# The MLP's up projection with the high and low part of x side by side

## Chip, cores and metric

One core of a Trainium2 chip runs the whole program. The metric is the device time of one execution in microseconds (us), as the median of several runs.

## The reference, cut to what matters

Two decoder layers work on x, 256 tokens of 1024 channels, in float32. The end of each layer is a squared-ReLU MLP with 4096 hidden channels:

```
hm = rmsnorm(x, norm_mlp[l])
x = x + jnp.square(jax.nn.relu(hm @ w_up[l])) @ w_down[l]
```

Before it stand the token mixers (a state-space branch, two attentions, gates, an output projection) and a cross attention. The state-space branch of the second layer needs tables that depend on parameters alone; the kernel computes them during the first layer's MLP.

## The kernel before

**Split products.** Each float32 matrix and each activation is split into a high part (rounded to `fp32r`) and a low part (the rest). A product is the sum of three: high x high, high x low, low x high (helper `three`, L1819 to L1821).

**Units and chunks.** All weights go through one pipeline. A unit is two chunks of 128 x 1024 values. SyncE loads a chunk into `raw`, ScalarE (ACT) rounds it into `w_hi` (L898), VectorE (DVE) subtracts to get `w_lo` (L1295), TensorE (PE) multiplies. `prep(u)` makes both chunks of a unit. `w_hi` has four slots, so ACT can round a chunk only once the chunk four places back (two units) has been multiplied.

**The MLP.** `up(g)` is two units, `("up", g, 0)` and `("up", g, 1)`; each makes 256 hidden channels for 256 tokens: 8 row tiles of x times 2 column tiles of the weights (`ft`) is 16 places, three matmuls of 256 columns each, 48 in all. `down(g)` is two units of 24 matmuls of 512 columns. The order is up(0), up(1), down(0), up(2), down(1), ..., up(7), down(6), down(7): 16 up and 16 down units a layer. In this text unit n is counted from up(0) = units 0 and 1; so up(1) is 2 and 3, up(2) 6 and 7, up(3) 10 and 11, up(4) 14 and 15, up(5) 18 and 19, up(6) 22 and 23, up(7) 26 and 27, and the rest are down units.

**Emptying an up unit.** The two column tiles of an up unit lie side by side in one PSUM bank, T0 for the first unit of a pair and T1 for the second. ACT copies the bank with Relu into `r_b` (which frees the bank), DVE squares it into `q_b`, ACT rounds that into `bT_hi`, DVE subtracts into `bT_lo`. ACT waits for the square inside the step, with everything else of ACT queued behind it.

**Order on the engines.** Each engine runs a list fixed by the program. For unit u of the MLP, ACT and DVE first prepare unit u + 2 and then empty unit u; after that come the side stages attached to u (`side_stages`). In the first layer's MLP these make the second layer's tables: `p_ct` after unit 10, `p_cv` (DVE) after 12 and 13, `p_b0` (DVE) after 15, `p_bv` (DVE) after 16 and 18, `p_k` after 20 and 21 (96 small PE matmuls into bank X0 after unit 20, 16 small ACT copies to `kt`, half after unit 20 and half after 21, the last of which frees X0), and `p_bt` after 22, 23, 24 and 25 (two each time: four PE transposes into X0 or X1, then an ACT copy that frees it). GpSimd (POOL) works on the same tables. The second layer's MLP has no side stages.

**Banks.** `USES` lists the users of a bank in program order, and `before` makes each user wait until the one ahead has freed the bank (on PE, ahead of its first matmul).

Of the kernel before, what the change touches and what calls it, by code (L numbers as in the profile page):

```python
# [30 lines left out]
P = 128  # L31
# [95 lines left out]
def side_stages(l):  # L127

    side = {u: [] for u in range(-1, NU)}

    def after(u, *stage):
        side[u].append(stage)

    up0 = AT_UNIT["up", 0, 0]
    if l:
        after(-1, "turn_x", "mix", 0)
        after(-1, "turn_x", "mix", 1)
    after(-1, "norm", "mix")
    if l == 0:
        after(-1, "p_dt", 0)  # L140
    after(-1, "stats", "mix", 0)
    after(-1, "stats", "mix", 1)
    if l == 0:
        after(-1, "p_angle", 0)
        after(-1, "p_cos", 0)
        after(2, "lam", 0)
        after(3, "lam", 1)
        after(4, "p_params", 0)
    after(1, "row")

    def pre(tgt, u):

        after(u["ct"], "p_ct", tgt)
        for r in range(2):
            after(u["cv"][r], "p_cv", tgt, r)
        after(u["b0"], "p_b0", tgt)
        for r in range(2):
            after(u["bv"][r], "p_bv", tgt, r)
        for n in range(2):
            after(u["k"][n], "p_k", tgt, n)  # L160
        for n in range(8):
            after(u["bt"][n // 2], "p_bt", tgt, n)

    if l == 0:
        pre(0, dict(ct=0, cv=(1, 2), b0=3, bv=(4, 5), k=(5, 6), bt=(6, 7, 7, 8)))
        first = FIRST[0]
        after(up0 + 6, "p_params", 1)
        after(up0 + 7, "p_dt", 1)
        after(up0 + 7, "p_angle", 1)
        after(up0 + 8, "p_cos", 1)  # L170
        pre(1, dict(ct=up0 + 10, cv=(up0 + 12, up0 + 13), b0=up0 + 15, bv=(up0 + 16, up0 + 18),
                    k=(up0 + 20, up0 + 21), bt=(up0 + 22, up0 + 23, up0 + 24, up0 + 25)))
    else:
        first = FIRST[1]
    for kb in range(4):
        after(first + kb, "ssm_in", kb)
        after(first + 2 + kb, "ssm_out", kb)
    after(first + 6, "gelu")
    after(first + 9, "gelu_split")

    for p in range(SB_PAIRS):
        after(6 + 2 * p, "sb_s", p)
        after(7 + 2 * p, "sb_u", p)
        after(8 + 2 * p, "sb_p", p)
    after(10, "rope", 0)
    after(15, "turn", 0)
    after(12, "rope", 1)
    after(15, "turn", 1)

    for j in range(2 * DA_HEADS):  # L190
        after(16 + j, "da_s", j)
        after(17 + j, "da_t", j)
        after(18 + j, "da_p", j)
    after(21, "da_c", 0)
    after(22, "da_n", 0)
    after(25, "da_o", 0)
    after(25, "da_c", 1)
    after(25, "da_n", 1)
    after(27, "da_o", 1)
    if l == 0:  # L200
        after(32, "stats", "mem", 0)
        after(32, "stats", "mem", 1)
    after(33, "mem_diag")
    after(34, "mem_row")
    for j in range(4):
        after(34 + j // 2, "mem_split", j)
    after(AT_UNIT["wout", 1], "stats", "cross", 0)
    after(AT_UNIT["wout", 3], "stats", "cross", 1)
    after(AT_UNIT["wout", 3], "turn_x", "cross", 0)
    after(AT_UNIT["xk", 0], "turn_x", "cross", 1)  # L210
    after(AT_UNIT["xk", 0], "norm", "cross")

    xq = AT_UNIT["xq", 0]
    for h in range(XA_HEADS):
        after(xq + h // 2, "xa_s", h)
        after(xq + 1 + h // 2, "xa_t", h)
    for h in range(XA_HEADS):
        after(xq + h // 2, "xa_w", h)
    for h in range(XA_HEADS):
        after(xq + 3, "xa_p", h)  # L220
    after(AT_UNIT["xo", 0], "stats", "mlp", 0)
    after(AT_UNIT["xo", 1], "turn_x", "mlp", 0)
    after(AT_UNIT["xo", 1], "turn_x", "mlp", 1)
    after(AT_UNIT["xo", 1], "norm", "mlp")
    after(AT_UNIT["xo", 1], "stats", "mlp", 1)
    for u in range(7, 27):
        side[u].sort(key=lambda s: RANK.get(s[0], 7))
    return side
# [12 lines left out]
def unit_banks(key):  # L241

    if key[0] == "u":
        return [["A0", "A2"][key[1]]]
    if key[0] in ("sq", "sk", "xk", "xq") or isinstance(key[0], tuple):
        return ["T0", "T1"][key[1] % 2:][:1]
    if key[0] in ("sv", "dq", "dk", "dv", "xv"):
        return ["T0", "T1"]
    if key[0] == "glu":
        return ["T0", "T1"] if key[1] else ["A0", "A1"]  # L250
    if key[0] == "branch":
        return {1: ["T0", "T1"], 2: ["A0", "A1"], 0: ["A2", "A3"]}[key[2]]
    if key[0] == "wout":
        return ["A0", "A1"] if key[1] < 2 else ["A2", "A3"]
    if key[0] == "xo":
        return ["A2", "A3"] if key[1] == 0 else ["A0", "A1"]
    if key[0] == "up":
        return ["T0", "T1"][key[2]:][:1]
    return ["A0", "A1"] if key[2] == 0 else ["A2", "A3"]


# [104 lines left out]
def hybrid_trunk(nc, a, out):  # L366
    with ExitStack() as ctx:
# [20 lines left out]
        raw = [nc.alloc_sbuf_tensor_at(f"s_raw{i}", [P, CW], F32, offset=ring + 4 * CW * i) for i in range(LO)]  # L388
        w_hi = [sb(f"w_hi{i}", [P, CW], F32R) for i in range(HI)]
        x = sb("x", [P, NT, D])  # L390
        hT_hi, hT_lo = sb("hT_hi", [P, KD, T], F32R), sb("hT_lo", [P, KD, T], F32R)

        bT_hi, bT_lo = sb("bT_hi", [P, 12, T], F32R), sb("bT_lo", [P, 12, T], F32R)
        gates = sb("gates", [P, 16, T])
# [117 lines left out]
        xmax_ready, xw_ready = signal("xmax_ready", XA_HEADS), signal("xw_ready", XA_HEADS)  # L512
        xo_hi = signal("xo_hi", XA_HEADS)
        NUP = 2 * (HIDDEN // 512)
        sq_made, hid_hi, hid_ready = signal("sq_made", NUP), signal("hid_hi", NUP), signal("hid_ready", NUP)

        act_order, dve_order, pool_order = sem("act_order"), sem("dve_order"), sem("pool_order")
# [24 lines left out]
        def f32(ap):  # L542
            return ap.bitcast(F32)
# [36 lines left out]
        def by_place(ap):  # L580

            return ap.rearrange("p (k b j) -> p k j b", b=NB, j=BL)

        def by_block(ap):
            return ap.rearrange("p (k j b) -> p k j b", b=NB, j=BL)
# [310 lines left out]
        def _(act):  # L896
# [6 lines left out]
            for l in range(DEPTH):  # L903
# [121 lines left out]
                def evac(u):  # L1025
# [29 lines left out]
                    elif key == ("glu", 0):  # L1055
                        gated(1)
                        fn(flat(gates[:, 0:8, :]), flat(gates[:, 0:8, :]), ACT.Sigmoid).then_inc(*st.sig(gate_ready))
                        for j, bk in enumerate(b):
                            act.wait_ge(*st.at(*freed(l, bk, key)))
                            fn(flat(hT_hi[:, 2 * j:2 * j + 2, :]), st_y[:, 0, 512 * j:512 * j + 512]).then_inc(*st.sig(glu_hi))  # L1060
                    elif kind == "branch":
                        cb, n = key[1:]
                        if cb == 0 and n == 1:
# [7 lines left out]
                        if n == 0:  # L1071
                            for j in range(2):
                                act.wait_ge(*st.at(mg_made, 2 * cb + j + 1))
                                fn(flat(merged(cb)[0][:, 2 * j:2 * j + 2, :]), macc(cb, j)).then_inc(*st.sig(mg_hi))
                    elif kind == "xq":
                        take(flat(qk[:, 2 * key[1]:2 * key[1] + 2, :]), b[0], key)
                    elif kind == "up":
                        g, i = key[1:]
                        if g:
                            act.wait_ge(*st.at(sq_made, 2 * g + i - 1))  # L1080
                        take(r_b[i], b[0], key, ACT.Relu)
                        act.wait_ge(*st.at(sq_made, 2 * g + i + 1))
                        if g >= 2:

                            act.wait_ge(*st.at(chunk_done, 2 * AT_UNIT["down", g - 2, 1] + 2))
                        k0 = 4 * (g % 2) + 2 * i
                        fn(flat(bT_hi[:, k0:k0 + 2, :]), q_b[i]).then_inc(*st.sig(hid_hi))
# [162 lines left out]
        def _(dve):  # L1250
# [39 lines left out]
            for l in range(DEPTH):  # L1290
# [230 lines left out]
                def evac(u):  # L1521
# [36 lines left out]
                    elif key == ("glu", 0):  # L1558
# [5 lines left out]
                                .then_inc(*st.sig(*freed(l, bk, key)))  # L1564
                        for j in range(2):
                            dve.wait_ge(*st.at(glu_hi, j + 1))
                            tt(flat(hT_lo[:, 2 * j:2 * j + 2, :]), st_y[:, 0, 512 * j:512 * j + 512],
                                      f32(flat(hT_hi[:, 2 * j:2 * j + 2, :])), ALU.subtract)\
                                          .then_inc(*st.sig(glu_ready))
                    elif kind == "branch":  # L1570
                        cb, n = key[1:]
# [15 lines left out]
                        if n == 0:  # L1587
                            for j in range(2):
                                dve.wait_ge(*st.at(mg_hi, 2 * cb + j + 1))
                                hi, lo = merged(cb)  # L1590
                                tt(flat(lo[:, 2 * j:2 * j + 2, :]), macc(cb, j),
                                          f32(flat(hi[:, 2 * j:2 * j + 2, :])), ALU.subtract)\
                                              .then_inc(*st.sig(mg_ready))
                    elif kind in ("wout", "xo", "down"):
                        residual(key, b)
                    elif kind == "up":
                        g, i = key[1:]
                        dve.wait_ge(*st.at(*freed(l, b[0], key)))
                        tt(q_b[i], r_b[i], r_b[i]).then_inc(*st.sig(sq_made))
                        dve.wait_ge(*st.at(hid_hi, 2 * g + i + 1))  # L1600
                        k0 = 4 * (g % 2) + 2 * i
                        tt(flat(bT_lo[:, k0:k0 + 2, :]), q_b[i], f32(flat(bT_hi[:, k0:k0 + 2, :])),
# [197 lines left out]
        def _(pe):  # L1800
# [14 lines left out]
            for l in range(DEPTH):  # L1815
# [48 lines left out]
                def unit(u, late):  # L1864
# [10 lines left out]
                    for half in range(2):  # L1875
# [4 lines left out]
                        if kind == "T":  # L1880
# [3 lines left out]
                            for k, ft in order:  # L1884
# [3 lines left out]
                                elif after_norm and ft == 0 and ks % 2 == 0:  # L1888
                                    pe.wait_ge(*st.at(*freed(l, TURN_BANKS[ks // 2], ("turn_x", after_norm, ks // 4))))
                                c = slice(ft * P, ft * P + P)  # L1890
                                o = bank[banks[ft // 2]][:, (ft % 2) * T:(ft % 2) * T + T]
                                ins = three(o, wh[:, k, c], wl[:, k, c], hi[:, ks, :], lo[:, ks, :],
                                            half == 0 and k == 0 and ft % 2 == 0, half == 1 and k == kt // 2 - 1,
# [272 lines left out]
```

## Time and profile before

| what | value |
|---|---|
| median of 3 runs | 1093.74 us (1093.61 to 1093.97) |
| the profiled execution's own time | 1096.48 us |
| its span in the trace | 1094.8 us |
| PE busy | 1029.5 us (94%) |
| DVE busy | 736.7 us (67%) |
| ACT busy | 573.4 us (52%) |
| first layer's MLP on PE | 376.4 to 568.5 us |
| second layer's MLP on PE | 905.5 us to near the end |

The span runs from the first to the last instruction of the trace; the own time is 1.7 us longer. A matmul's row is longer than its share of PE, since matmuls overlap: what one costs is the distance from its start to the next one's.

### The profile page before, as it was taken

How to read it: one execution, taken by the hardware profiler on the slowest of the kernel's cores; microseconds unless marked ns; L12 is line 12 of the kernel's file. 1: busy time of each engine (PE TensorE's matmuls, PEld its weight loads, DVE VectorE, ACT ScalarE, POOL GpSimd, SP SyncE). 2: the span in 40 equal slices, each digit the busy share in tenths (PEclk: the TensorE clock that was granted, in tenths of full speed). 3: DMA queues.
4: the chain of work that ended last, by engine and by line, in shares of the span. 5: the costliest groups of instructions: out<-in, count | busy, mean ns of one | idle time of the engine just before them, and what ended most of it. 6: DMA issues, size and time to landing. Idle time of an engine off the chain costs nothing. (4 is left out here: it accounts for less than half of the span.)

```text
span 1094.8 us, 18335 instructions
## 1 busy us (share of the span) xinstructions
PE 1029.5 (94%) x7096; PEld 937.9 (86%) x7096; DVE 736.7 (67%) x1061; ACT 573.4 (52%) x868; POOL 176.7 (16%) x304
## 2 busy tenths in 40 slices
PE   5778999999999899999989999999999989999996
PEld 4766889989998799988979878998998979899995
DVE  4884975878875565887465579478787647555554
ACT  6446445546765555546554454554637546444442
POOL 5993300000000003997000011000000000000000
PEclk9889999999999999999999999999999999999998
DMA  7253336645554366654556543465565445666661
GB/s 281 97 173 95 98 120 194 201 141 174 176 175 149 96 232 182 189 172 136 172 173 189 163 130 97 135 213 154 155 181 175 146 135 160 190 189 192 182 188 74
DMA packets 58022, 177.21 MB, mean 162 GB/s; under 512 B 14160, under 2 KB 16208, under 8 KB 57680
## 3 DMA queue, kind: packets, MB, share of 16 engines
q1 hardware_dynamic: 57792, 176.04, 52.2%
q8 instruction: 57, 0.93, 0.3%
q14 instruction: 29, 0.24, 0.1%
q10 hardware_dynamic: 144, 0.00, 0.0%
HBM read 172.87 MB, written 3.15 MB: 161 GB/s over the span
## 5 line engine op out<-in xcount | busy, mean ns | idle before, releaser
L1295 DVE TENSOR_TENSOR s_w_lo<-s_raw,s_w_hi 128x1024 fp32r<-128x1024 f32 x312 | 377.3, 1238 | 146.7 <-ACT s_w_hi L898 143.0
L898 ACT ACTIVATE s_w_hi<-s_raw 128x1024 fp32r<-128x1024 f32 x312 | 321.0, 1054 | 215.2 <-PE p_T L1821 130.5
L1819 PE MATMUL p_T<-s_hT_hi,s_w_hi 128*128 128x256 f32 x1088 | 313.4, 288 | 12.0 <-DVE s_w_lo L1295 11.9
L1820 PE MATMUL p_T<-s_hT_lo,s_w_hi 128*128 128x256 f32 x1088 | 310.0, 285 | 0.0
L1821 PE MATMUL p_T<-s_hT_hi,s_w_lo 128*128 128x256 f32 x1088 | 309.7, 285 | 0.0
L1819 PEld LDWEIGHTS p_T<-s_hT_hi,s_w_hi 128*128 128x128 f32 x1088 | 210.7, 194 | 17.6 <-issue 16.2
L1820 PEld LDWEIGHTS p_T<-s_hT_lo,s_w_hi 128*128 128x128 f32 x1088 | 210.8, 194 | 0.4
L1821 PEld LDWEIGHTS p_T<-s_hT_hi,s_w_lo 128*128 128x128 f32 x1088 | 210.9, 194 | 0.0
L1819 PE MATMUL p_A<-s_w_hi,s_bT_hi 128*128 128x512 f32 x320 | 125.2, 391 | 2.4 <-DVE s_bT_lo L1295 2.4
L1820 PE MATMUL p_A<-s_w_lo,s_bT_hi 128*128 128x512 f32 x320 | 124.7, 390 | 0.0
L1821 PE MATMUL p_A<-s_w_hi,s_bT_lo 128*128 128x512 f32 x320 | 124.6, 389 | 0.0
L1819 PEld LDWEIGHTS p_A<-s_w_hi,s_bT_hi 128*128 128x128 f32 x320 | 60.1, 188 | 15.2 <-issue 3.2
L1821 PEld LDWEIGHTS p_A<-s_w_hi,s_bT_lo 128*128 128x128 f32 x320 | 60.1, 188 | 12.7
L1820 PEld LDWEIGHTS p_A<-s_w_lo,s_bT_hi 128*128 128x128 f32 x320 | 60.1, 188 | 11.7
L727 POOL TENSOR_TENSOR s_small<-s_small 128x16 f32<-128x16 f32 (+1 forms) x130 | 59.8, 483 | 10.2 <-ACT s_small L898 7.8
L1819 PE MATMUL p_T<-s_w_hi,s_hT_hi 128*128 128x512 f32 x128 | 52.2, 408 | 8.0 <-issue 8.0
L898 ACT ACTIVATE s_bT_hi<-s_att 128x512 fp32r<-128x512 f32 x32 | 20.2, 632 | 58.5 <-DVE s_att L1295 58.5
L1821 PE MATMUL p_T<-s_w_hi,s_hT_lo 128*128 128x512 f32 x128 | 50.8, 397 | 0.0
L1820 PE MATMUL p_T<-s_w_lo,s_hT_hi 128*128 128x512 f32 x128 | 50.7, 396 | 0.0
L727 POOL TENSOR_TENSOR s_small<-s_col,s_small 128x16 f32<-128x16 f32 x4 | 1.2, 313 | 296.7 <-ACT s_small L898 296.7
L1819 PE MATMUL p_A<-s_hT_hi,s_w_hi 128*128 128x256 f32 x128 | 37.8, 295 | 9.5 <-DVE s_hT_lo L1394 9.5
L1819 PE MATMUL p_T<-s_bT_hi,s_w_hi 128*128 128x256 f32 x160 | 45.9, 287 | 0.3 <-issue 0.3
(263 smaller groups left out, 1685.5 us busy)
## 6 DMA issues: line engine op xcount, KB each, us to landing
s_raw<-in_weights SPq DMA_DIRECT2D x312, 512.0 KB, 3.6
s_bt<-in_mem_t SPq DMA_DIRECT2D x2, 1024.0 KB, 6.1
s_st_y<-in_x_t SPq DMA_DIRECT2D x2, 512.0 KB, 6.9
s_x<-in_x SPq DMA_DIRECT2D x1, 1024.0 KB, 10.6
s_vN<-in_ssm_bc SPq DMA_DIRECT2D x2, 512.0 KB, 8.9
u_turn<-s_st_y SPq DMA_DIRECT2D x4, 256.0 KB, 3.8
s_uB<-u_turn SPq DMA_DIRECT2D x8, 128.0 KB, 3.4
s_bt<-in_mem SPq DMA_DIRECT2D x1, 1024.0 KB, 5.9
```

Source lines behind the costliest of these rows:

```text
L727: return nc.gpsimd.tensor_tensor(o, i0, i1, op)
L898: return nc.scalar.activation(o, i, f, **kw)
L1295: return V.tensor_tensor(o, i0, i1, op)
L1819: mm(o, lhi, rhi, start=first, stop=False, **kw)
L1820: mm(o, lhi, rlo, start=False, stop=False, **kw)
L1821: return mm(o, llo, rhi, start=False, stop=last, **kw)
```

## The change

`hT_hi` and `hT_lo` become two halves of one tile, so that for each of the 8 row tiles of x the high and the low part of its 256 tokens are 512 neighbouring columns. In an up unit each place has two products in place of three: `w_hi` times both parts (512 columns, a whole bank), and `w_lo` times the high part (256 columns, added to the bank's first half). The result is the sum of the two halves of the bank. So each column tile needs a bank of its own: the first unit of a pair takes T0 and T1, the second X0 and X1. Emptying: ACT copies the second half of each bank (256 columns each, no Relu) into `r_b`, DVE adds the first half of each bank to it (which frees the bank) and then takes max(r, 0) times r in one `scalar_tensor_tensor`. As X0 and X1 have other users, the stage `p_bt` moves from after units 22, 23, 24, 25 to after 24, 25, 28, 29. All else keeps its order; some access patterns are written in three dimensions for the new tile.

```
 pre(1, ...
-        bt=(up0 + 22, up0 + 23, up0 + 24, up0 + 25)))
+        bt=(up0 + 24, up0 + 25, up0 + 28, up0 + 29)))
 unit_banks:
-        return ["T0", "T1"][key[2]:][:1]
+        return ["T0", "T1"] if key[2] == 0 else ["X0", "X1"]
 tiles:
-        hT_hi, hT_lo = sb("hT_hi", [P, KD, T], F32R), sb("hT_lo", [P, KD, T], F32R)
+        hT = sb("hT", [P, KD, 2, T], F32R)
+        hT_hi, hT_lo = hT[:, :, 0, :], hT[:, :, 1, :]
 ACT, evac of "up":
-        take(r_b[i], b[0], key, ACT.Relu)
+        act.wait_ge(*st.at(chunk_done, 2 * u + 2))
+        for j, bk in enumerate(b):
+            ins = fn(r_b[i][:, j * T:j * T + T], bank[bk][:, T:2 * T])
+            ins.then_inc(*st.sig(up_copied)) if j else ins.then_inc(*st.mid())
         act.wait_ge(*st.at(sq_made, 2 * g + i + 1))
 DVE, evac of "up":
-        dve.wait_ge(*st.at(*freed(l, b[0], key)))
-        tt(q_b[i], r_b[i], r_b[i]).then_inc(*st.sig(sq_made))
+        dve.wait_ge(*st.at(up_copied, 2 * g + i + 1))
+        for j, bk in enumerate(b):
+            tt(r_b[i][:, j * T:j * T + T], r_b[i][:, j * T:j * T + T], bank[bk][:, 0:T], ALU.add)\
+                .then_inc(*st.sig(*freed(l, bk, key)))
+        dve.wait_ge(*st.mine())
+        V.scalar_tensor_tensor(out=q_b[i], in0=r_b[i], scalar=0.0, in1=r_b[i], op0=ALU.max, op1=ALU.mult)\
+         .then_inc(*st.sig(sq_made))
 PE, unit:
+        if key[0] == "up":
+            o = bank[banks[ft]]
+            mm(o[:, :], wh[:, k, c], hT[:, ks, :, :].rearrange("p r n -> p (r n)"),
+               start=(half == 0 and k == 0), stop=False, skip_group_check=True)
+            ins = mm(o[:, 0:T], wl[:, k, c], hi[:, ks, :], start=False,
+                     stop=(half == 1 and k == kt // 2 - 1), skip_group_check=True)
+            continue
```

## Rows read from the trace of the kernel before

**Rows 1.** Page, engines: busy us (share of the span) xinstructions.
```profile
PE 1029.5 (94%) x7096; PEld 937.9 (86%) x7096; DVE 736.7 (67%) x1061; ACT 573.4 (52%) x868; POOL 176.7 (16%) x304
```

**Rows 2.** Windows of the MLPs: length, then busy us (xcount) of each engine, clock, DMA.
```profile
core 0: us, PE busy (x) PEld busy (x) DVE busy (x) ACT busy (x) POOL busy (x), PEclk, DMA share, GB/s
444.00:504.00 60.00, 58.21 (x430) 51.09 (x429) 52.97 (x54) 26.43 (x32) 57.80 (x80) 1.00 0.58 170
905.00:1063.00 158.00, 157.94 (x1060) 146.37 (x1059) 92.31 (x100) 78.78 (x98) 0.00 (x0) 1.00 0.61 183
```

**Rows 3.** Timeline, PE, second layer: first matmul of up, down and up again.
```profile
939.48 0.28 PE L1819 MATMUL p_T<-s_hT_hi,s_w_hi 128*128 128x256 f32 x1
...
950.99 0.40 PE L1819 MATMUL p_A<-s_w_hi,s_bT_hi 128*128 128x512 f32 x1
...
961.89 0.28 PE L1819 MATMUL p_T<-s_hT_hi,s_w_hi 128*128 128x256 f32 x1
```

**Rows 4.** Groups by line and shape: xcount, busy us, mean ns, idle before.
```profile
L1295 DVE TENSOR_TENSOR s_w_lo<-s_raw,s_w_hi 128x1024 fp32r<-128x1024 f32 x312 | 377.3, 1238 | 146.7 <-ACT s_w_hi L898 143.0 <-DVE s_att L1295 0.6 <-DVE s_w_lo L1295 0.6
L1295 DVE TENSOR_TENSOR s_att<-s_att 128x512 f32<-128x512 f32 x36 | 24.8, 688 | 0.5 <-DVE s_w_lo L1295 0.4
...
L1295 DVE TENSOR_TENSOR s_att<-p_X,s_masks 128x256 f32<-128x256 f32 x32 | 12.8, 420 | 8.6 <-PE p_X L1998 5.3 <-PE p_X L2032 2.7 <-DVE s_vN L1535 0.4
...
L1713 DVE SCALAR_TENSOR_TENSOR s_att<-s_att 128x768 f32<-128x768 f32 x8 | 8.0, 1005 | 6.9 <-ACT s_att L898 6.9
...
L1295 DVE TENSOR_TENSOR s_att<-s_vN,s_small 128x768 f32<-128x768 f32 x4 | 3.7, 963 | 3.4 <-POOL s_small L727 3.2
...
L898 ACT ACTIVATE s_att<-p_T 128x512 f32<-128x512 f32 x32 | 18.5, 579 | 0.0
...
L898 ACT ACTIVATE s_bT_hi<-p_A 128x256 fp32r<-128x256 f32 x16 | 6.1, 383 | 6.1 <-PE p_A L2089 5.8
```

**Rows 5.** Timeline, DVE, first layer's MLP; s_att rows are the squares of up units.
```profile
386.02 0.69 DVE L1295 TENSOR_TENSOR s_att<-s_att 128x512 f32<-128x512 f32 x1
...
445.92 2.38 DVE L1295 TENSOR_TENSOR s_w_lo<-s_raw,s_w_hi 128x1024 fp32r<-128x1024 f32 x2 [2.65 <-ACT s_w_hi L898]
448.23 0.70 DVE L1295 TENSOR_TENSOR s_att<-s_att 128x512 f32<-128x512 f32 x1
...
465.55 0.71 DVE L1295 TENSOR_TENSOR s_att<-s_att 128x512 f32<-128x512 f32 x1
...
470.29 0.70 DVE L1295 TENSOR_TENSOR s_att<-s_att 128x512 f32<-128x512 f32 x1
...
489.50 0.69 DVE L1295 TENSOR_TENSOR s_att<-s_att 128x512 f32<-128x512 f32 x1
...
500.76 0.70 DVE L1295 TENSOR_TENSOR s_att<-s_att 128x512 f32<-128x512 f32 x1
```

**Rows 6.** Timeline, ACT: rounding after p_ct; the second half of p_k's copies.
```profile
444.73 2.01 ACT L898 ACTIVATE s_w_hi<-s_raw 128x1024 fp32r<-128x1024 f32 x2
...
509.71 3.61 ACT L898 ACTIVATE s_kt<-p_X 32x512 f32<-32x512 f32 x8
```

**Rows 7.** Timeline, PE: units 18, p_k, 21, 22, p_bt, p_bt, 24.
```profile
478.05 0.36 PE L1819 MATMUL p_T<-s_hT_hi,s_w_hi 128*128 128x256 f32 x1 [0.20 <-DVE s_w_lo L1295]
...
497.01 0.64 PE L1931 MATMUL p_X<-s_ct,s_tmp 128*32 128x128 f32 x16
...
500.08 0.50 PE L1819 MATMUL p_A<-s_w_hi,s_bT_hi 128*128 128x512 f32 x1
...
505.66 0.28 PE L1819 MATMUL p_T<-s_hT_hi,s_w_hi 128*128 128x256 f32 x1
...
513.47 1.06 PE L1804 MATMUL p_X<-s_ident,s_gates 128*128 128x128 f32 x8 [1.90 <-ACT s_kt L898]
...
521.61 1.03 PE L1804 MATMUL p_X<-s_ident,s_gates 128*128 128x128 f32 x8
522.40 0.48 PE L1819 MATMUL p_A<-s_w_hi,s_bT_hi 128*128 128x512 f32 x1
```

**Rows 8.** Window of unit 23, columns as in rows 2.
```profile
514.00:522.00 8.00, 8.00 (x57) 8.00 (x56) 4.95 (x5) 4.98 (x8) 1.09 (x2) 0.79 0.27 89
```

More of the change, by code:

```diff
@@ L171, in side_stages @@
         pre(1, dict(ct=up0 + 10, cv=(up0 + 12, up0 + 13), b0=up0 + 15, bv=(up0 + 16, up0 + 18),
-                    k=(up0 + 20, up0 + 21), bt=(up0 + 22, up0 + 23, up0 + 24, up0 + 25)))
+                    k=(up0 + 20, up0 + 21), bt=(up0 + 24, up0 + 25, up0 + 28, up0 + 29)))
     else:
@@ L514, in hybrid_trunk @@
         NUP = 2 * (HIDDEN // 512)
+        up_copied = signal("up_copied", NUP)
         sq_made, hid_hi, hid_ready = signal("sq_made", NUP), signal("hid_hi", NUP), signal("hid_ready", NUP)
@@ L582, in by_place, with by_tile @@
             return ap.rearrange("p (k b j) -> p k j b", b=NB, j=BL)
+        def by_tile(ap):
+            return ap.rearrange("p (k n) -> p k n", n=T)
         def by_block(ap):
@@ L1059, in evac @@
                             act.wait_ge(*st.at(*freed(l, bk, key)))
-                            fn(flat(hT_hi[:, 2 * j:2 * j + 2, :]), st_y[:, 0, 512 * j:512 * j + 512]).then_inc(*st.sig(glu_hi))
+                            fn(hT_hi[:, 2 * j:2 * j + 2, :], by_tile(st_y[:, 0, 512 * j:512 * j + 512])).then_inc(*st.sig(glu_hi))
                     elif kind == "branch":
@@ L1073, in evac @@
                                 act.wait_ge(*st.at(mg_made, 2 * cb + j + 1))
-                                fn(flat(merged(cb)[0][:, 2 * j:2 * j + 2, :]), macc(cb, j)).then_inc(*st.sig(mg_hi))
+                                fn(merged(cb)[0][:, 2 * j:2 * j + 2, :], by_tile(macc(cb, j))).then_inc(*st.sig(mg_hi))
                     elif kind == "xq":
@@ L1566, in evac @@
                             dve.wait_ge(*st.at(glu_hi, j + 1))
-                            tt(flat(hT_lo[:, 2 * j:2 * j + 2, :]), st_y[:, 0, 512 * j:512 * j + 512],
-                                      f32(flat(hT_hi[:, 2 * j:2 * j + 2, :])), ALU.subtract)\
+                            tt(hT_lo[:, 2 * j:2 * j + 2, :], by_tile(st_y[:, 0, 512 * j:512 * j + 512]),
+                                      f32(hT_hi[:, 2 * j:2 * j + 2, :]), ALU.subtract)\
                                           .then_inc(*st.sig(glu_ready))
@@ L1590, in evac @@
                                 hi, lo = merged(cb)
-                                tt(flat(lo[:, 2 * j:2 * j + 2, :]), macc(cb, j),
-                                          f32(flat(hi[:, 2 * j:2 * j + 2, :])), ALU.subtract)\
+                                tt(lo[:, 2 * j:2 * j + 2, :], by_tile(macc(cb, j)),
+                                          f32(hi[:, 2 * j:2 * j + 2, :]), ALU.subtract)\
                                               .then_inc(*st.sig(mg_ready))
```

## The prediction

> **What bounds the kernel now.** I read the page's first part, then the windows of the two MLPs, then PE's timeline there, and last the timelines of DVE and ACT where PE has gaps. PE is busy for 94% of the span, DVE for 67% [rows 1]. That average hides two kinds of stretch. In the second layer's MLP, PE is busy for 157.94 of 158 us while DVE works 92.31 [rows 2]: the distance between matmuls alone sets the pace. In the first layer's MLP from 444 to 504 us, DVE is busy for 52.97 of 60 us [rows 2]; what is left are pauses of about 0.7 us in which it waits for ACT's rounding of an up unit. There DVE, with the table work, is the bound, and PE shows it: unit 18 is held for `w_lo` [rows 7]. So each edit must be asked twice, once where PE paces and once where DVE does.
>
> **Part 1, PE's matmuls.** Two up units are 96 matmuls of 256 columns and take 950.99 - 939.48 = 11.51 us, 119.9 ns each; two down units are 48 of 512 columns and take 961.89 - 950.99 = 10.90 us, 227.1 ns each [rows 3]. Two narrow ones cost 239.8, so a matmul has a fixed part of 239.8 - 227.1 = 12.7 ns, and that is all the change takes away: a place costs 227.1 + 119.9 = 347.0 ns after 359.7. An up unit has 16 places: 0.20 us. The columns stay what they were. All 32 up units would give 6.5 us. Bounds: 512-wide matmuls right after a narrow stretch start a little dearer (PE needs 505.66 - 500.08 = 5.58 us for the 24 of unit 21 [rows 7], 232.5 ns each), which would leave 7.3 ns a place; if the fixed part went altogether, a place would gain 38 ns. I take 12.7, since both widths show it over dozens of matmuls with a weight load each.
>
> A page speaks against this term. The Trainium skill, "TensorE: Matmul & The Clock Gate", section "Back-to-back issue gap", gives N / 2.4 + 2.5 ns for an isolated matmul with N columns at full clock. By it a place would gain 2.5 ns and the 32 units 1.3 us. The trace does not agree: 119.9 ns for 256 columns, where the page's form gives 109.2. It stands as a rival below.
>
> **Part 2, DVE's work per up unit.** Before: one square of 512 elements, 688 ns. After: two additions of 256 elements with one operand in PSUM, and one `scalar_tensor_tensor` of 512. The nearest row for an addition is 420 ns (256 elements from PSUM). Instructions in a row overlap by about 0.1 us (two `w_lo` take 2.38 [rows 5], one 1.238 [rows 4]), so the pair takes 0.74. The third must wait for the second's result; 0.03 for that. A `scalar_tensor_tensor` of 768 elements takes 1005 ns where a plain one takes 963 [rows 4]: 0.04 more. So 0.8 us more DVE time per up unit. Below, 0.5: the additions at half a square each, overlapping fully with what surrounds them. Above, 1.1: the additions stretched as `w_lo` is in places while POOL works. ACT has two copies of 383 ns, overlapping, for one of 579 [rows 4]: 0.1 us more, hidden behind DVE's `w_lo`, which ends later.
>
> **Part 3, second layer.** An up unit takes PE 5.56 us, and DVE needs 2 x 1.19 (`w_lo`), 0.7 + 0.8, the 0.7 pause and 0.7 (`bT_lo`), 5.3 in all; after two up units two down units follow with 2.4 us each, so DVE falls behind by little and catches up, two units ahead of need. No wait appears. A new wait on banks is possible only at the start, where up(1) needs T0 and T1 one unit after up(0) filled them. In the first layer the square of unit 0 starts at 386.02 [rows 5]; additions there would be done by 386.8, and unit 2 starts at 387.6. It passes. Second layer: 16 x 0.20 = -3.2 us.
>
> **Part 4, first layer up to p_k.** PE gains 0.20 in each of units 0, 1, 2, 3, 6, 7, 10: it is 1.4 us early at the end of unit 10. From there on the order of ACT and DVE counts. Emptying unit 10 costs 0.8 more, so ACT reaches `p_ct` and then the rounding of 444.73 [rows 6] 0.6 early, and DVE starts the `w_lo` of 445.92 [rows 5] 0.6 early. From there to 500.76 DVE has no slack that a later PE or ACT could give back. Each emptying puts 0.8 on it: unit 11 (448.23) makes it 0.2 late, unit 14 (465.55) 1.0, unit 15 (470.29) 1.8, unit 18 (489.50) 2.6 [rows 5]. The emptying of unit 19 then starts at 500.76 + 2.6 = 503.4. PE's own gains in units 11 to 19 are worth nothing here: unit 18 starts 1.8 late, at about 479.9 after 478.05 [rows 7], with PE idle for some 4 us.
>
> **Part 5, the new wait.** `p_k` writes X0 on PE after unit 20, and X0 now has a user just ahead: unit 19, up(5)'s second. Before, PE began `p_k` at 497.01 [rows 7], 3.7 us before the square of unit 19 even began. Now it must wait for unit 19's first addition, which ends at 503.4 + 0.4 = 503.8. PE reaches that point near 498.7 (unit 19 can start at 487.5, when its `w_lo` is made, then 5.6 and 5.5 us) and stands for about 5 us. Queued behind it are unit 21 and all that follows. `p_k` takes 500.08 - 497.01 = 3.1 us [rows 7]. After such a pause the clock is low for a while: in the window of unit 23, which follows a pause of 1.90 us [rows 7], it was 0.79 of full over 8 us, so 8 x 0.21 = 1.7 us were lost [rows 8]. What a low clock costs `p_k`'s small matmuls no row shows: between 0.2 and 1.8 us in all; I take 1.0. Unit 21 starts at 503.8 + 3.1 + 1.0 = 507.9, where it started at 500.08.
>
> **Part 6, from unit 21 on.** Before, PE waited again: from the end of unit 22 to 513.47 for ACT's copies of `p_k` [rows 6, 7], and then ran unit 23 slow. This wait goes: the copies of the second half end about when unit 22 does. So units 21, 22, 23 follow closely, 5.6 us each: unit 23 ends at 507.9 + 16.7 = 524.6 after 521.61 [rows 7], 3.0 late. The step of `p_bt` takes 522.40 - 521.61 = 0.8 us each time [rows 7]; before, three of four came after this point, now all four: +0.8. Units 26 and 27 give back 0.4. X0 and X1 are free in time for unit 27 (the copies of 0.6 us run beside unit 26) and for the stages after 28 and 29. Late at the layer's end: 3.0 + 0.8 - 0.4 = 3.4 us.
>
> **Sum.** +3.4 - 3.2 = +0.2 us. The profiled execution of 1096.48 us (span 1094.8) would become 1096.7. It lies 2.7 us above the median of the runs shown; on the median the same difference gives 1094.0 us.
>
> **Rivals.**
>
> *A, the gain comes through.* The additions hide in the pauses and `p_k`'s wait is short. For it: DVE's share is 67%, and pauses of 0.7 us stand beside each emptying. Against: those pauses wait for ACT's rounding, which waits for the very step that grows. In full: -6.5 us, 1087.2. Chance 0.12.
>
> *B, the wait at p_k costs more than the fixed part brings.* Its place is X0 between units 19 and 21. An emptying at 1.1 us puts 5 x 0.3 = 1.5 us on the chain, and a low clock through `p_k` and the start of unit 21 another 0.8: +2.5 us, 1096.2. It decides once unit 21 starts later than about 509.9. For it: POOL is busy for 57.80 of these 60 us [rows 2] beside DVE. Chance 0.29.
>
> *C, a matmul's fixed part is not saved.* By the page's 2.5 ns, or because a wide matmul in this mix is dearer, as in unit 21, the second layer gives 0.6 in place of 3.2, and the chain begins 0.3 early in place of 1.4, with 0.3 more for units 26 and 27: +4.2 us, 1097.9. Chance 0.05.
>
> The forecast has the remaining 0.54.
>
> **How the numbers follow.** A measurement of this kernel tells 0.2% (2.2 us) from no change. Below 1091.6 lie A with 0.12 and the low end of my own sum (emptying 0.5 us, which takes 1.5 off, and a place gaining more than 12.7 ns) with 0.09: faster 0.21. Above 1095.9 lie most of B (0.25), C (0.05) and 0.02 of the forecast: slower 0.32. Same: 0.47. The likeliest case alone runs from 1091.9 (0.5 us, low clock 0.2) to 1095.6. The range leaves out most of A, the upper end of C: 1091.0 to 1097.6.
>
> **What would show it.** In the second layer's MLP, two up units at 11.1 us after 11.51, with no wait on PE: part 1 and 3. If they are near 11.4, C is right. In the first layer, PE waiting several us ahead of L1931's counterpart for DVE's write of `s_att`: part 5; no such wait, and A is right. The start of unit 23 with no wait for `s_kt`: part 6. Four additions near 0.42 us for each pair of units: part 2. The prediction is wrong if the first layer's MLP ends within 1 us of its old place or more than 6 us late.

## The result and the profile after

The changed kernel takes 1100.91 us (median of 4 runs, 1100.23 to 1102.26) against 1093.86 for before: ratio 1.0064, 95% interval 1.0046 to 1.0081. It is slower by 0.6%. The forecast was no change at 1094.0 us; the time lies outside its range, which ended at 1097.6.

The profiled execution took 1102.26 us, with a span of 1100.2 us against 1094.8 before: 5.4 us more. The page's first part stands beside [rows 1]:

```profile
PE 1029.2 (94%) x6584; PEld 911.6 (83%) x6584; DVE 760.3 (69%) x1125; ACT 574.4 (52%) x900; POOL 176.5 (16%) x304
```

512 matmuls fewer, PE's busy time as before, DVE busy for 24 us more. Where the span grew is read from PE's timeline. In each execution I take two lengths: the first layer's MLP from its first up matmul to the first transpose of x behind it, and the second layer's from its first up matmul to the first matmul of down(6), which follows the last up unit.

| stretch | before | changed | difference |
|---|---|---|---|
| first layer's MLP | 192.06 us | 198.17 us | +6.1 us |
| second layer's MLP (up to down(6)) | 157.62 us | 155.68 us | -1.9 us |

The MLP starts 1.0 us later in this execution; that belongs to no stage of the change (over all the kernels below, whose programs are alike up to there but for the tile of x's parts, this start lies anywhere from 375.3 to 378.3 us). The stages sum to +4.2 us of the 5.4, and with the later start to 5.2; the stretch between the two MLPs (337.0 and 337.2 us) and the one behind them (31.7 in both) are as before.

**Second layer.** Timeline of PE, changed kernel: first matmul of two up units, then of the down unit behind them. It answers to [rows 3].

```profile
946.04 0.39 PE L1906 MATMUL p_T<-s_hT,s_w_hi 128*128 128x512 f32 x1
...
957.33 0.40 PE L1832 MATMUL p_A<-s_w_hi,s_bT_hi 128*128 128x512 f32 x1
```

11.29 us for two up units, after 11.51: 0.11 us a unit gained, where 0.20 was forecast.

**DVE's longer emptying.** Groups by line and shape of the changed kernel, DVE and ACT (xcount, busy us, mean ns, idle before), to set beside [rows 4]:

```profile
L1611 DVE SCALAR_TENSOR_TENSOR s_att<-s_att 128x512 f32<-128x512 f32 x32 | 22.7, 710 | 1.1
...
L1303 DVE TENSOR_TENSOR s_att<-s_att,p_X 128x256 f32<-128x256 f32 x32 | 11.9, 414 | 0.0
...
L903 ACT ACTIVATE s_att<-p_T 128x256 f32<-128x256 f32 x32 | 10.2, 373 | 0.0
```

An addition takes 414 ns where 420 was estimated, and the last operation 710 ns, 22 over the square of before (688) where 40 was estimated.

**First layer.** Timeline of PE in the changed kernel: start of unit 18, of `p_k`, of units 21, 22, 23 and 24 [compare rows 7]; the bracket is the idle time before and what ended it.

```profile
481.48 0.47 PE L1906 MATMUL p_T<-s_hT,s_w_hi 128*128 128x512 f32 x1 [3.65 <-DVE s_w_lo L1303]
...
504.94 0.87 PE L1951 MATMUL p_X<-s_ct,s_tmp 128*32 128x128 f32 x12 [4.45 <-DVE s_att L1303]
...
510.04 0.80 PE L1832 MATMUL p_A<-s_w_hi,s_bT_hi 128*128 128x512 f32 x1
...
516.83 0.39 PE L1906 MATMUL p_T<-s_hT,s_w_hi 128*128 128x512 f32 x1
...
522.47 0.40 PE L1906 MATMUL p_X<-s_hT,s_w_hi 128*128 128x512 f32 x1
...
528.12 0.40 PE L1832 MATMUL p_A<-s_w_hi,s_bT_hi 128*128 128x512 f32 x1
```

The wait that was forecast ahead of `p_k` is there, 4.45 us long and ended by DVE's write of `s_att`. DVE's timeline has what ended it, the first of unit 19's two additions [compare the last of rows 5]:

```profile
504.39 0.74 DVE L1303 TENSOR_TENSOR s_att<-s_att,p_X 128x256 f32<-128x256 f32 x2
```

But `p_k` then takes 510.04 - 504.94 = 5.1 us, and unit 21 516.83 - 510.04 = 6.8 us; before they took 3.1 and 5.6. The windows of these stretches, columns as in [rows 2], show why:

```profile
505.00:510.00 5.00, 5.00 (x96) 3.15 (x96) 4.07 (x5) 2.52 (x3) 4.92 (x4) 0.50 0.01 3
510.00:513.00 3.00, 3.00 (x16) 2.36 (x9) 2.04 (x1) 2.64 (x6) 2.88 (x2) 0.55 0.00 0
```

The granted clock is 0.50 in `p_k`, the lower of TensorE's two levels, and still 0.55 in the first 3 us of unit 21.

### The profile page after: what moved, and what is told of

The parts are those of the page before. It is cut to its first block and busy times, and to the rows that moved or that the text cites. A ratio compares the mean times of both kernels' runs of the same rounds, so it can differ in the third digit from the quotient of the medians.

```text
span 1100.2 us, 17437 instructions
## 1 busy us (share of the span) xinstructions
PE 1029.2 (94%) x6584; PEld 911.6 (83%) x6584; DVE 760.3 (69%) x1125; ACT 574.4 (52%) x900; POOL 176.5 (16%) x304
## 5 line engine op out<-in xcount | busy, mean ns | idle before, releaser
L1832 PE MATMUL p_T<-s_hT,s_w_hi 128*128 128x256 f32 x576 | 167.0, 290 | 9.4 <-DVE s_w_lo L1303 9.4
L1833 PE MATMUL p_T<-s_hT,s_w_hi 128*128 128x256 f32 x576 | 163.8, 284 | 0.0
L1834 PE MATMUL p_T<-s_hT,s_w_lo 128*128 128x256 f32 x576 | 163.8, 284 | 0.0
L1832 PEld LDWEIGHTS p_T<-s_hT,s_w_hi 128*128 128x128 f32 x576 | 111.3, 193 | 13.6 <-issue 12.5
L1833 PEld LDWEIGHTS p_T<-s_hT,s_w_hi 128*128 128x128 f32 x576 | 111.5, 194 | 0.1
L1834 PEld LDWEIGHTS p_T<-s_hT,s_w_lo 128*128 128x128 f32 x576 | 111.3, 193 | 0.0
L1906 PE MATMUL p_T<-s_hT,s_w_hi 128*128 128x512 f32 x256 | 92.5, 403 | 3.8 <-DVE s_w_lo L1303 3.7
L1906 PE MATMUL p_X<-s_hT,s_w_hi 128*128 128x512 f32 x256 | 90.8, 397 | 0.3 <-DVE s_w_lo L1303 0.3
L1908 PE MATMUL p_T<-s_hT,s_w_lo 128*128 128x256 f32 x256 | 72.5, 283 | 0.0
L1908 PE MATMUL p_X<-s_hT,s_w_lo 128*128 128x256 f32 x256 | 71.8, 281 | 0.0
L1906 PEld LDWEIGHTS p_T<-s_hT,s_w_hi 128*128 128x128 f32 x256 | 48.8, 190 | 16.3 <-issue 4.6
L1832 PE MATMUL p_T<-s_w_hi,s_hT 128*128 128x512 f32 x128 | 52.4, 409 | 9.5 <-issue 9.5
```

The source lines that it names most:

```text
L1832: mm(o, lhi, rhi, start=first, stop=False, **kw)
L1833: mm(o, lhi, rlo, start=False, stop=False, **kw)
L1834: return mm(o, llo, rhi, start=False, stop=last, **kw)
L1906: mm(o[:, :], wh[:, k, c], hT[:, ks, :, :].rearrange("p r n -> p (r n)"), start=(half == 0 and k == 0), stop=False, skip_group_check=True)
L1908: ins = mm(o[:, 0:T], wl[:, k, c], hi[:, ks, :], start=False, stop=(half == 1 and k == kt // 2 - 1), skip_group_check=True)
```

## The experiments

My theory after the traces had three parts. DVE's additions make its queue late in the stretch where it is the bound. Bank X0 makes PE stand in that queue ahead of `p_k`. The low clock behind that wait costs 3.2 us. The rivals were that one of these alone explains it, or the new places do. All kernels are compared with before; the columns at the right are from their profiled executions.

| kernel | ratio to before (95%) | first MLP, us | second MLP, us |
|---|---|---|---|
| before | 1 | 192.06 | 157.62 |
| changed | 1.0064 (1.0046 to 1.0081) | 198.17 | 155.68 |
| e1_place | 1.0001 (0.9987 to 1.0016) | 192.16 | 157.61 |
| e2_dvework | 1.0060 (1.0044 to 1.0075) | 196.74 | 157.61 |
| e3_fill | 1.0024 (1.0014 to 1.0034) | 194.79 | 156.09 |
| e4_pklate | 1.0035 (1.0022 to 1.0048) | 196.38 | 155.67 |
| e5_l1only | 0.9985 (0.9975 to 0.9995) | 192.12 | 156.03 |
| e6_most | 0.9990 (0.9976 to 1.0003) | 191.70 | 156.09 |
| e7_l0only | 1.0079 (1.0063 to 1.0094) | 198.32 | 157.62 |
| e8_grouped | 1.0043 (1.0027 to 1.0060) | 196.68 | 155.31 |
| e9_after_bv | 1.0024 (1.0012 to 1.0035) | 192.89 | 156.08 |
| e10_before_bv | 0.9980 (0.9971 to 0.9990) | 188.54 | 157.62 |
| e11_most_grouped | 0.9983 (0.9974 to 0.9993) | 190.00 | 155.20 |
| e12_most_bv | 0.9951 (0.9938 to 0.9963) | 187.94 | 155.30 |

**e1_place: the banks and the moved stage without the rest.**

```
-        return ["T0", "T1"][key[2]:][:1]
+        return ["T0", "X0"][key[2]:][:1]
-        bt=(up0 + 22, up0 + 23, up0 + 24, up0 + 25)
+        bt=(up0 + 24, up0 + 25, up0 + 28, up0 + 29)
```

> The kernel before with the new places alone: the second up unit of a pair fills one bank X0 in place of T1, and p_bt stands after units 24, 25, 28, 29. Matmuls, ACT's Relu and DVE's square are as before. Theory (the loss needs both DVE's longer emptying and the bank X0): ACT's Relu frees X0 near 493.5 us, before PE reaches p_k near 497, so there is no wait ahead of p_k; the time is within 1 us of before. Rival (the places themselves cost, as more users queue on X0): PE waits ahead of p_k or p_bt for X0, and it is 4 us or more slower.

Measured: ratio 1.0001, first MLP 192.16 us. PE starts `p_k` at 496.96 with no wait, so the new places cost nothing by themselves. The wait for ACT's copies of `p_k` that before had ahead of `p_bt` stands now ahead of unit 23, 1.84 us after 1.90.

**e2_dvework: DVE's work without the rest.**

```
-                        tt(q_b[i], r_b[i], r_b[i])
+                        for j in range(2):
+                            half = r_b[i][:, j * T:j * T + T]
+                            tt(half, half, half, ALU.max).then_inc(*st.mid())
+                        dve.wait_ge(*st.mine())
+                        V.scalar_tensor_tensor(out=q_b[i], in0=r_b[i], scalar=0.0, in1=r_b[i], op0=ALU.max, op1=ALU.mult)
```

> The kernel before with DVE's longer emptying alone: two extra in-place operations of 256 elements (a max of r_b with itself, all in SBUF) ahead of the square, and the square as scalar_tensor_tensor. Banks, matmuls and stages as before. Theory (DVE is the bound between 446 and 501 us of the first layer, 0.8 us for each of six emptyings): unit 18 waits about 3 us longer, ACT's copies of p_k end about 5 us later, the first layer's MLP is 4 to 6 us longer, the second layer's unchanged: +5 us. Rival (the additions hide beside PE, and the loss comes from the bank): within 1 us of before.

Measured: ratio 1.0060, first MLP +4.7 us, second unchanged at 157.61. Timeline of PE: unit 18 and the first `p_bt`.

```profile
481.29 0.55 PE L1824 MATMUL p_T<-s_hT_hi,s_w_hi 128*128 128x256 f32 x1 [3.68 <-DVE s_w_lo L1295]
...
518.94 0.74 PE L1809 MATMUL p_X<-s_ident,s_gates 128*128 128x128 f32 x5 [2.45 <-ACT s_kt L898]
```

Unit 18's wait is 3.68 us, in the changed kernel 3.65, before 0.20: that part of the loss is DVE's work alone. The 4.7 us are even a low figure: behind the 2.45 us wait the clock stayed at 1.00 and unit 23 took 5.84 us, where before it fell behind a wait of 1.90 us and the same unit took 7.32 (521.61 - 514.29 [rows 7]). The window of unit 23 in e2_dvework, columns as in [rows 2]:

```profile
519.76:525.60 5.84, 5.84 (x52) 5.84 (x51) 4.42 (x6) 3.41 (x6) 0.00 (x0) 1.00 0.29 80
```

So DVE's work is the larger part of the loss; the new banks put a dearer wait ahead of `p_k`, but they also do away with the one ahead of unit 23. The second layer, with the same additions and no table work, does not feel them.

**e3_fill: PE at work in place of the wait.** Ahead of the wait for X0 in `p_k` of the second table:

```
+                        if t == 1:
+                            pe.wait_ge(*st.at(*freed(l, "T0", ("up", 5, 0))))
+                            for _ in range(20):
+                                mm(bank["T0"][:, :], hT_hi[:, 0, 0:P], hT[:, 0, :, :].rearrange("p r n -> p (r n)"), ...)
                         pe.wait_ge(*st.at(*before(l, b, s)))
```

> The changed kernel with 20 matmuls of 512 columns into the empty bank T0 ahead of p_k's wait for X0, so that PE is at work in place of waiting for 4.45 us; their result is not used. Theory (a low clock after the wait made p_k take 5.1 us after 3.1, and unit 21 6.8 after 5.6): p_k takes 3.1 and unit 21 5.6 us, and the kernel is 3.2 us faster than the changed one, about 3.8 us slower than before. Rival (the small matmuls of p_k are slow for another reason, as being late among POOL's and DVE's work): p_k and unit 21 stay as they are, and so does the time.

Measured: ratio 1.0024 after 1.0064, which is 4.4 us where 3.2 were expected; the first MLP is 3.4 us shorter than in the changed kernel. Timeline of PE: the added matmuls, `p_k`, unit 21, unit 22.

```profile
498.99 0.62 PE L1950 MATMUL p_T<-s_hT 128*128 128x512 f32 x2
...
503.62 0.65 PE L1956 MATMUL p_X<-s_ct,s_tmp 128*32 128x128 f32 x16
...
506.69 0.50 PE L1832 MATMUL p_A<-s_w_hi,s_bT_hi 128*128 128x512 f32 x1
...
512.26 0.39 PE L1906 MATMUL p_T<-s_hT,s_w_hi 128*128 128x512 f32 x1
```

`p_k` takes 3.07 and unit 21 5.57 us, both as before. Nothing else that unit 21 waits for was changed, and `p_k` starts 0.15 us earlier, counted from the MLP's start. So the low clock cost 5.10 - 3.07 and 6.79 - 5.57, 3.2 us in all: shown.

**e4_pklate: p_k away from unit 19.**

```
-        k=(up0 + 20, up0 + 21), bt=(up0 + 24, up0 + 25, up0 + 28, up0 + 29)
+        k=(up0 + 24, up0 + 25), bt=(up0 + 28, up0 + 29, up0 + 30, up0 + 30)
```

> The changed kernel with p_k moved from after units 20 and 21 to after 24 and 25, and p_bt to after 28, 29, 30, 30, so that unit 19's emptying does not stand ahead of p_k. Theory: no wait ahead of p_k; units 19 to 23 follow w_lo alone, unit 23 ends 7 to 8 us earlier; p_k's 3.1 us come later, and two pairs of p_bt in a row cost about 1 us: 3 to 4 us faster than the changed kernel, 3 to 4 us slower than before. Rival (DVE's late work alone sets this stretch, the bank only shows it): the wait moves to w_lo of units 21 and 22, and the time stays within 1 us of the changed kernel's.

Measured: ratio 1.0035, first MLP 1.8 us shorter than in the changed kernel; 3 to 4 were expected. The wait ahead of `p_k` is gone, and another has come ahead of unit 21:

```profile
502.62 0.47 PE L1832 MATMUL p_A<-s_w_hi,s_bT_hi 128*128 128x512 f32 x1 [2.58 <-DVE s_w_lo L1303]
```

The low clock came with it. Window of unit 21, from its first matmul to unit 22's, columns as in [rows 2]:

```profile
502.62:509.77 7.15, 7.14 (x24) 5.72 (x25) 6.22 (x7) 3.48 (x4) 6.99 (x5) 0.76 0.25 76
```

7.15 us, where unit 21 took 5.58 before. And one of the `p_bt` now waits 1.05 us for ACT. So both readings hold in part: the bank made the wait longer, but DVE's queue stands behind it, holds PE at the next `w_lo`, and the clock falls there too.

**e5_l1only, e6_most, e7_l0only: the change in one part of the up units.** A function chooses the form, and both forms stand in the code:

```
+def wide_up(l, g):
+    return l == 1                # e5;  e6: l == 1 or g <= 2;  e7: l == 0
-        return ["T0", "T1"] if key[2] == 0 else ["X0", "X1"]
+        if not wide_up(l, key[1]):
+            return ["T0", "T1"][key[2]:][:1]
+        return ["T0", "T1"] if key[2] == 0 else ["X0", "X1"]
```

(`p_bt` is where it was in e5 and e6, and as in the changed kernel in e7.)

> The change in the second layer alone; the first layer's up units, banks and stages are as before (with the new tile for x's parts). Theory (a place gains 6.8 ns on PE, measured in the changed kernel, and where PE paces DVE's additions are free): 16 units x 0.11 us, 1.8 us faster than before, and the first layer's MLP takes as long as before. Rival (the second layer's gain is eaten by something at its edges, or the new tile costs elsewhere): no faster than before.

> The change in the second layer and in the first layer's up(0) to up(2), that is in all up units before DVE becomes the bound; p_bt where it was. Theory: 22 units x 0.11 us, 2.4 us faster than before, no wait ahead of p_k. Rival (three longer emptyings before the bound stretch delay the tables' start): the first layer gives back its 0.6 us and it equals the kernel with the second layer alone.

> The change in the first layer alone. Theory: the whole loss stands here, so it is the changed kernel without the second layer's gain: 1.8 us slower than that, about 8.8 us slower than before. Rival (part of the loss is in the second layer or in the tile's layout): less than 7 us slower than before.

Measured: the second layer alone is 0.15% faster (0.9985, 0.9975 to 0.9995), its MLP 1.6 us shorter, the first layer's as before. The first layer alone is slower than the whole change (1.0079), with a first MLP of 198.32 us. The loss is all there, as expected. e6 shortens the first MLP by 0.4 us of the 0.7 expected and has no wait ahead of `p_k`; its time, 0.9990 (0.9976 to 1.0003), can't be told from before or from e5.

**e8_grouped: the order of wide and narrow matmuls.**

```
                                     mm(o[:, :], wh[:, k, c], hT[:, ks, ...], ...)
+                                    lows = [(k, ks)]
+                                    if not after_norm:
+                                        lows = [(q, s0 + half * (kt // 2) + q) for q in range(kt // 2)] if k == kt // 2 - 1 else []
+                                    for q, qs in lows:
+                                        ins = mm(o[:, 0:T], wl[:, q, c], hi[:, qs, :], ...)
```

> The changed kernel with another order of an up unit's matmuls (not in the first unit of a layer): for each column tile and chunk first the four of 512 columns, then the four of 256, in place of one by one. Same matmuls, same weight loads. Theory (a wide matmul costs 232 ns where it alternates with narrow ones, and 227 among its like): an up unit takes 5.56 us after 5.65, and the kernel is about 2.5 us faster than the changed one. Rival (the 5 ns come from something else, as the place of the operands in memory): 5.65 us as now.

Timeline of PE, second layer, first matmul of two up units and of the down unit behind them:

```profile
945.24 0.61 PE L1906 MATMUL p_T<-s_hT,s_w_hi 128*128 128x512 f32 x2
...
956.44 0.40 PE L1832 MATMUL p_A<-s_w_hi,s_bT_hi 128*128 128x512 f32 x1
```

11.20 us for two up units: 5.60 a unit, between the 5.65 of the changed kernel and the 5.56 expected. Alternating costs part of what is missing. The first MLP is 1.5 us shorter, but most of that is luck of the clock: here it was back by the end of `p_k`, and unit 21 took 5.6 us. So the whole kernel's 1.0043, 2.3 us below the changed kernel where 2.5 were expected, says little on the grouping.

**e9_after_bv, e10_before_bv: less DVE work ahead of unit 19.** In e9 on the changed kernel, in e10 on the one before (with `p_bt` after 24, 25, 28, 29):

```
-        bv=(up0 + 16, up0 + 18)
+        bv=(up0 + 16, up0 + 22)
```

> The changed kernel with the second half of p_bv (5.9 us of DVE) moved from after unit 18 to after unit 22, so that it no longer stands ahead of unit 19's emptying. Theory (the wait ahead of p_k is DVE's queue of work, and the bank makes PE stand in it): unit 19's first addition ends about 5.9 us earlier, PE reaches p_k with no wait and at full clock, p_k takes 3.1 and unit 21 5.6 us; the first layer's MLP takes 190.6 us after 198.2, and the kernel is 7 to 8 us faster than the changed one, about as before or 0.5 us faster. Rival (the late work is only pushed to units 23 to 25, where w_lo then comes late): less than 4 us faster than the changed one.

> The kernel before with the same move of p_bv, and p_bt after 24, 25, 28, 29 (its tables must be made first). Theory: its wait for the copies of p_k and the low clock behind it go, the first layer's MLP takes 188.5 us after 192.1, 3.6 us faster than before; so once this stage is relieved the change is worth about nothing in the first layer, where unit 18 still waits longer for w_lo, and 1.9 us in the second. Rival (the wait moves on): within 1 us of before.

Measured: in e9 PE starts `p_k` at 500.31 with no wait and at full clock, and the first MLP is 5.3 us shorter than in the changed kernel, not 7.6. The rest is a new wait, where unit 23's emptying is late behind the moved work and `p_bt` needs its bank (behind this wait the clock stayed at 1.00):

```profile
528.12 1.07 PE L1817 MATMUL p_X<-s_ident,s_gates 128*128 128x128 f32 x8 [2.22 <-DVE s_att L1303]
```

By the ratios the whole kernel is 4.4 us faster than the changed one, where 7 to 8 were expected, and 0.24% slower than before.

e10 came out as worked out: 188.54 us (188.5 expected), 0.20% faster than before (0.9980, 0.9971 to 0.9990). That went against one expectation: with the stage relieved in both, the change still costs 192.89 - 188.54 = 4.4 us in the first layer, since unit 18 (3.8 us) and now `p_bt` still wait for DVE.

**e11_most_grouped, e12_most_bv: the versions that the findings point to.** e11 is e6 with the order of e8; e12 adds the move of e10.

> The change where PE sets the pace only (second layer, and up(0) to up(2) of the first), with an up unit's matmuls in groups of four wide and four narrow ones. Theory: 0.16 us for each of 22 units, 3 us faster than before. Rival (the gain of the grouping was the clock's chance alone): as the same kernel without the grouping, 2 us or less.

> The one before with the moved p_bv, and p_bt after 24, 25, 28, 29. Theory: both gains add, 3.0 + 3.6 us, 6 to 7 us faster than before, the fastest of all. Rival (they overlap in the stretch from 446 to 515 us): no faster than the kernel before with the moved p_bv by more than 1.5 us.

Measured: e11 0.9983 (0.9974 to 0.9993), which is about 1.9 us and short of the 3 expected, though its second MLP is 2.4 us shorter. Most of the 1.7 us by which its first MLP is below e6's is luck of the clock again: with the same code in both, unit 23 took 5.84 us here and 7.09 in e6. e12 1089.32 us, 0.9951 (0.9938 to 0.9963): 5.4 us faster than before, its interval clear of e10's, though 6 to 7 were expected. It is faster than both kernels.

## Why the prediction was wrong

The waits came where they were forecast. One term was too small by far, the price of the low clock behind the wait at `p_k`, and one gain too large, that of a matmul's fixed part.

- **Part 1, the fixed part of a matmul.** Forecast 12.7 ns a place, 0.20 us a unit; measured 0.11 us a unit in steady state [against rows 3]. A wide and a narrow matmul in turn cost 11.29 / 32, 352.8 ns, not the 347.0 that the two cost among their like. e8 shows that the alternation is part of that. The 2.5 ns that the Trainium skill gives for an isolated matmul ("TensorE: Matmul & The Clock Gate", "Back-to-back issue gap") would have given 0.04 us a unit, which is too small: the truth lies between the two. In the second layer this is -1.9 us where -3.2 was forecast.
- **Part 2, DVE's work.** Forecast 0.8 us an emptying; measured 0.74 for the two additions and 22 ns more for the square: right.
- **Part 3, no wait in the second layer.** Right: the traces of all kernels have none there, and e2 shows the additions to be free there.
- **Part 4, the chain.** Forecast: unit 18 starts 1.8 us late. Measured: 481.48 - 478.05, less the 1.0 by which this MLP starts late, 2.4 us. Unit 19's additions were forecast at 503.4 and came at 504.39, less 1.0. That this fits to the tenth is in part luck: DVE's row of 445.92 came at 447.08, less 1.0, which is 0.8 later than forecast, and some of its later rows ran shorter than before, as the last two of `p_bv` (2.47 us for both at 499.08, where those at 494.52 and 496.07 took 1.52 and 1.53). e2 shows that DVE's work alone makes the wait of unit 18.
- **Part 5, the wait at p_k.** Forecast: first addition done at 503.8, a stand of about 5 us. Measured: done at 504.80 less 1.0, and 4.45 us. e1 shows that the bank without the additions makes no such wait, e9 that less DVE work takes it away. **The step that failed is the price of the clock behind it:** "between 0.2 and 1.8 us in all; I take 1.0". It was 5.1 - 3.1 for `p_k` and 6.8 - 5.6 for unit 21, 3.2 us, and e3 gives it back. That is 2.2 over the value taken and 1.4 over the upper bound. The prediction had no row for either figure. Its one row of a low clock, unit 23 behind 1.90 us [rows 8], already lost 1.7 us with only the 0.8 us of a `p_bt` between; here the small matmuls of `p_k` ran at 0.50, took two thirds longer, and unit 21 then began at the low clock too, where part 6 counts it at 5.6 us.
- **Part 6.** The wait for the copies of `p_k` went, as forecast, and each `p_bt` took 0.8 us. Late at the end of the layer: 6.1 us, 3.4 forecast. 2.2 of the difference are the clock; the rest is mostly the smaller gain of a place in units 22, 23, 26 and 27.

With what the two MLPs measured, the sum is +6.1 - 1.9 = +4.2 us in place of +0.2. The profiled executions differ by 5.8 us in their own time, and the medians by 7.0. The 1 to 3 us beyond the stages are not explained: times less stages are +2.8 us for the changed kernel, +2.4 for e7 and e8, +3.3 for e9, +2.6 for e11, +0.8 to +1.9 for e2, e3, e4, e6, e10 and e12, and none for e1 and e5. The layout of the new tile is not needed for it, as e2 and e10 do not have it. Two things are seen to vary between profiled executions: the start of the first MLP (by 3.0 us) and the clock behind the waits of about 2 us. And the four executions of before in this comparison lie low: its 21 to 24 executions beside the experiments have medians of 1095.1 to 1095.4 us, which would leave 5.5 to 5.8 us for the change. No run here tells how much each gives.

Of the rivals, B named the right place and one of the two causes that it gave. The low clock was dearer than in the forecast, and by more than B has: 3.2 us, where B comes to 1.0 + 0.8. Its other cause, an emptying of 1.1 us, did not come: that took 0.80. And its sign, unit 21 starting later than about 509.9, did not show either: the start was at 510.04 less 1.0. The signs named in the forecast's last part fared likewise: two up units took 11.29 us, about halfway between 11.1 and 11.4, and the first layer's MLP ended 6.1 us late, just past the 6 that were to make the prediction wrong. A (the gain comes through) is refuted by e2 and e7. C is half true: the fixed part is saved, but only about half of it.

## What to carry to other kernels

Ask of a change where each engine is the bound, stretch by stretch: the same additions were free in one layer and cost 4.7 us in the other, and the kernel is best when the change is made only where its cover exists. A result buffer that is emptied at the end of a busy engine's queue must not be the one that the next small stage on the main engine needs. And count a pause of the matmul engine at more than its length: here the stage of small matmuls behind it ran slow and handed the slow clock on, so a pause of 4.45 us cost 7.7. Give that price as a range, for it is not the same each time: behind waits of about 2 us the clock fell in some of these executions and not in others. A comparison of two profiles must look at this before it names a cause.

## What the runs showed of the hardware

- The small matmuls of `p_k` (128 x 32 and 32 x 32 weights, 96 rows) take 3.07 us at full clock and 5.1 at the low one (changed kernel, e7_l0only), and the clock stayed at 0.50 through all of them; in e8_grouped they took 5.02 us and it came back at their end. Twenty matmuls of 512 columns ahead of them kept it at full.
- Whether a wait of about 2 us costs the clock differs between executions. The granted clock went to 0.50 behind waits of 1.90 us (before), 1.84 (e1_place) and 2.58 (e4_pklate), and stayed at 1.00 behind 1.92 (e11_most_grouped), 2.22 (e9_after_bv) and 2.45 (e2_dvework). All waits of 3.6 us and more inside the first layer's MLP had the low clock about them. Unit 23 took 7.32 us with the low clock (before) and 5.84 without (e2_dvework, e11_most_grouped).
- A matmul has a fixed cost beside its columns: 12.7 ns by the pitches of 256 and 512 columns among their like. Where the two alternate a pair costs 352.8 ns, 5.8 more than the two among their like (347.0), and 350.0 (11.20 / 32) when they stand in groups of four. But some up units ran at 5.55 us in place of 5.65 with the same code (the second pair of the second layer's MLP in the changed kernel, 11.09 us); what makes them faster is open.
